# An attention layer's Z projection as seven products, exponentials, last gate group and row factors moved, on one Trainium2 core

## What is computed

```python
h = rms_norm(x, g_mix)
(qa, ka, va, za, beta_in, a_in, qd, kd, vd, gate_a, gate_b) = split(h @ w_in)
qa, ka, va = silu(causal_depthwise_conv([qa, ka, va], conv_w))        # then l2-normalised q, k
oa = rms_norm(gated_delta_rule(qa, ka, va, beta, g), g_delta_out) * silu(za)
qd, kd = rms_norm(qd, q_norm), rms_norm(kd, k_norm)
od = rms_norm(diff_attention(qd, kd, vd, lam, rel_bias), g_subln) * (1 - lam_init)
mix = sigmoid(gate_a + b_gate[0]) * oa + sigmoid(gate_b + b_gate[1]) * od
x = x + mix @ w_o
x = x + moe_ffn(rms_norm(x, g_ffn), w_router, ..., w_up, w_down, ...)  # top 4 of 32, clamped SwiGLU
```

## Time and profile before

| | |
|---|---|
| median of three runs | 1276.15 us |
| profiled execution | 1277.58 us |
| its span (first to last instruction) | 1275.9 us |
| TensorE, matmuls | 1220.6 us, 96% of the span |
| VectorE | 391.1 us, 31% |
| ScalarE | 308.3 us, 24% |
| GpSimd | 43.3 us, 3% |
| moved by DMA | 465.59 MB, 365 GB/s over the span |
| chain that ended last | TensorE 65%, DMA 19%, VectorE 5%, ScalarE 3% |

### The profile page before, as it was taken

One profiled execution on the slowest core, in us unless ns is written; L12 is line 12 of the kernel. 1 busy time (PEld: TensorE's weight loads), 2 busy tenths in 40 slices (PEclk: granted clock), 3 DMA queues, 4 the chain that ended last, 5 costly groups with the idle time before them and its releaser, 6 DMA issues.

```text
span 1275.9 us, 14962 instructions
## 1 busy us (share of the span) xinstructions
PE 1220.6 (96%) x5558; PEld 535.2 (42%) x5558; DVE 391.1 (31%) x1041; ACT 308.3 (24%) x644; POOL 43.3 (3%) x100
## 2 busy tenths in 40 slices
PE   9999999999999999999999999999999999999997
PEld 7777456644443333333333333333333333333332
DVE  5776647479341221111221111221111112211111
ACT  3332222464222121121121112121121211111121
POOL 4401000000000000000000000000000000000000
PEclk9999999999999999999999999999999999999999
DMA  7644974698969999999999999999999999999997
GB/s 257 185 156 131 226 234 150 156 299 303 380 257 423 426 429 428 429 428 428 428 429 427 429 429 429 428 428 427 429 429 428 428 427 429 428 429 428 429 426 303
DMA packets 67582, 465.59 MB, mean 365 GB/s; under 512 B 11016, under 2 KB 14216, under 8 KB 42848
## 3 DMA queue, kind: packets, MB, share of 16 engines
q1 hardware_dynamic: 61768, 452.68, 86.1%
q0 software_dynamic: 5344, 11.95, 4.9%
q10 hardware_dynamic: 440, 0.58, 0.1%
HBM read 462.84 MB, written 1.97 MB: 364 GB/s over the span
## 4 chain that ended last, share of the span: by engine, by line
PE 65%; DMA 19%; DVE 5%; ACT 3%; issue 2%; SPq 1%; DVEq 0%; ACTq 0%
PE pb L2037 20%; DMA space<-in_w_up_dram 19%; PE pb L2084 14%; PE pb L1747 6%; PE pb L1978 4%; PE pb L1698 4%; PE pb L1678 3%; PE pb L1965 3%; PE pb L1892 2%; PE pb L1653 2%; PE pb L1972 1%; PE pb L1997 1%; DVE buf_a L1592 1%; DVE buf_a L1589 1%; DVE buf_a L1586 1%
## 5 line engine op out<-in xcount | busy, mean ns | idle before, releaser
L2037 PE MATMUL pb<-space,buf_a 128*64 128x512 f32 x2048 | 460.4, 595 | 16.1 <-DMA space<-in_w_up_dram 16.1
L2037 PEld LDWEIGHTS pb<-space,buf_a 128*64 128x64 f32 x2048 | 146.1, 137 | 285.3 <-issue 257.2
L1586 DVE TENSOR_SCALAR buf_a<-pb 128x256 f32<-128x256 f32 x64 | 26.9, 421 | 687.2 <-PE pb L2037 687.2
L2084 PE MATMUL pb<-space 128*64 128x512 f32 x1024 | 227.1, 595 | 7.3 <-ACT space L1114 7.3
L2084 PEld LDWEIGHTS pb<-space 128*64 128x64 f32 x1024 | 70.7, 137 | 140.9 <-issue 125.3
L1090 ACT ACT_TABLE_LOAD x32 | 41.1, 1283 | 222.4 <-PE pb L1965 222.4
L1678 PE MATMUL pb<-space 128*128 128x256 f32 x384 | 88.6, 384 | 1.0 <-ACT space L924 0.6
L1107 ACT ACTIVATE buf_a<-buf_a 128x256 f32<-128x256 f32 x64 | 26.7, 417 | 217.3 <-DVE buf_a L1586 217.3
L1678 PEld LDWEIGHTS pb<-space 128*128 128x128 f32 x384 | 71.3, 190 | 13.2 <-issue 2.4
L1116 ACT COPY space<-pb 128x512 f32<-128x512 f32 x32 | 18.7, 585 | 209.9 <-PE pb L2084 209.9
L1978 PE MATMUL pb<-space 64*128 64x512 f32 x264 | 65.6, 615 | 0.8 <-ACT space L1116 0.8
(11 more groups left out here) (322 smaller groups left out, 949.7 us busy)
## 6 DMA issues: line engine op xcount, KB each, us to landing
space<-in_w_up_dram SPq DMA_DIRECT2D x127, 2048.0 KB, 24.9
space<-in_w_down_dram SPq DMA_DIRECT2D x61, 2048.0 KB, 23.3
space<-in_w_in_dram SPq DMA_DIRECT2D x25, 1024.0 KB, 7.3
space<-in_w_in_dram SPq DMA_DIRECT2D x7, 2048.0 KB, 11.1
space<-in_w_in_dram POOLq DMA_DIRECT2D x8, 1024.0 KB, 10.7
space<-in_w_o_dram SPq DMA_DIRECT2D x4, 1024.0 KB, 5.2
space<-in_w_down_dram SPq DMA_DIRECT2D x4, 1024.0 KB, 29.2
xt<-in_x_dram SPq DMA_DIRECT2D x4, 512.0 KB, 8.9
```

The source lines that it names most:

```text
L1586: v.tensor_scalar(glu[:, cols], pairs[:, :, 0], LIMIT, None, ALU.min).then_inc(s_glu, 1)
L2037: ins = mm(up_out(hf, n_), xg[:, c, :], up_columns(line, hf, n_), start=False, stop=(c == KC - 1), skip_group_check=True)
L2084: ins = mm(pb[64 * hf:64 * hf + 64, 2, :], actT[:, c // 4 * 2 + c % 2, hf_in, :], slot(m)[:, at_:at_ + 512], start=(c == 0), stop=(c == KC ...
```

## The change

- Z joins `SEVEN`. Its products go in the order P5 P1 P3 P6 P2 P7 P4, in banks 0 and 1. ScalarE takes the products P5, P3, P1 and P7 out of PSUM, times 0.25, into `gz`, VectorE adds or subtracts the others (`results_step`, L1266 to L1279), ScalarE takes the tanh of each output and VectorE forms the product. Its weights are loaded as those of the other groups, with one first sum, one third sum and two growing sums. The list of products is one shorter (43 in place of 44), Z at index 22, GA at 29, GB at 36.
- `PLACES`, `BANKS` and `W_O_PLACES` have new entries; GA and GB use banks 0 to 3 in another order, and the quarters of `w_o` lie in other halves of slots 8 and 9. SP's order of loads follows. Slot 9 is freed with slot 8, at the fourth product of the output projection.
- Every item of the delta rule stands one index later, and so do attention's items and `odn`.
- The exponentials are an item of their own, `ex`, one index behind the scores and, on ScalarE, behind the copy of the turned weights of the head before.
- `odn`: ScalarE multiplies each block and head with its rows' factor (twelve and four operations, L1010), then VectorE multiplies with the gain, one operation a row block (L1454).
- GB goes in the order P5 P1 P2 P6 P3 P7 P4, with outputs ready in the order of `LAST_OUTS` (2, 1, 0, 3), so both of b = 0 first; the mixed rows' second half of b = 0 is turned ahead of P4 and the first half behind it.
- SP waits for GB's P7 before it loads `xt`.

```diff
 UNITS = ("P5", "P1", "P7", "P6", "P3", "P2", "P4")
+Z_UNITS = ("P5", "P1", "P3", "P6", "P2", "P7", "P4")
+LAST_UNITS = ("P5", "P1", "P2", "P6", "P3", "P7", "P4")
 HALVES = tuple((b, n, hf) for n in range(2) for b in range(NB) for hf in range(2))
-SEVEN = (KD, VD, GA, GB)
-SEQ = [(g, name) for g in range(6) for name in (UNITS if g in SEVEN else HALVES)]
+SEVEN = (KD, VD, Z, GA, GB)
+SEQ = [(g, name) for g in range(6) for name in {QD: HALVES, Z: Z_UNITS, GB: LAST_UNITS}.get(g, UNITS)]
...
 BANKS = {KD: {"P5": 0, "P3": 0, "P1": 7, "P6": 7, "P7": 6, "P4": 6, "P2": 1},
          VD: {"P5": 0, "P3": 0, "P1": 1, "P6": 1, "P7": 6, "P4": 6, "P2": 7},
-         GA: {"P5": 0, "P3": 0, "P1": 2, "P6": 2, "P7": 3, "P4": 3, "P2": 1},
-         GB: {"P5": 0, "P3": 0, "P1": 1, "P6": 1, "P7": 3, "P4": 3, "P2": 2}}
+         Z: {"P5": 0, "P3": 0, "P2": 0, "P4": 0, "P1": 1, "P6": 1, "P7": 1},
+         GA: {"P5": 2, "P3": 2, "P1": 3, "P6": 3, "P7": 1, "P4": 1, "P2": 0},
+         GB: {"P5": 2, "P3": 2, "P1": 0, "P6": 0, "P7": 1, "P4": 3, "P2": 3}}
...
 PLACES = {KD: {"T": (6, 0), "T3": (6, 1), "B11": (8, 0), "B22": (8, 1), "B21": (9, 0)},
           VD: {"T": (9, 1), "T3": (6, 1), "B11": (8, 0), "B22": (8, 1), "B21": (9, 0)},
-          Z: {(0, 0): (6, 0), (1, 0): (8, 0), (0, 1): (6, 1), (1, 1): (8, 1)},
-          GA: {"T": (9, 0), "T3": (6, 0), "B11": (9, 1), "B22": (8, 0), "B21": (8, 1)},
-          GB: {"T": (6, 1), "T3": (6, 0), "B11": (9, 1), "B22": (8, 0), "B21": (8, 1)}}
-W_O_PLACES = {(0, 0): (9, 0), (0, 1): (9, 1), (1, 0): (8, 0), (1, 1): (8, 1)}
+          Z: {"T": (6, 0), "T3": (6, 1), "B11": (8, 0), "B22": (8, 1), "B21": (9, 0)},
+          GA: {"T": (9, 1), "T3": (6, 1), "B11": (8, 0), "B22": (8, 1), "B21": (9, 0)},
+          GB: {"T": (6, 0), "T3": (6, 1), "B11": (8, 0), "B22": (8, 1), "B21": (9, 0)}}
+W_O_PLACES = {(0, 0): (9, 1), (0, 1): (8, 0), (1, 0): (9, 0), (1, 1): (8, 1)}
...
+Z_OUTS, LAST_OUTS = (1, 2, 0, 3), (2, 1, 0, 3)
...
-put(12, ("n2", 0))
...
+put(13, ("n2", 0))
...
 for h in range(H):
-    put(19 + 2 * h, ("a1", h))
-    put(21 + 2 * h, ("aw", h))
-    put(22 + 2 * h, ("a2", h))
-    put(23 + 2 * h, ("a3", h))
-put(35, ("odn", 0, 6))
-put(38, ("odn", 6, 8))
+    put(20 + 2 * h, ("a1", h))
+    put(21 + 2 * h, ("ex", h))
+    put(22 + 2 * h, ("aw", h))
+    put(23 + 2 * h, ("a2", h))
+    put(24 + 2 * h, ("a3", h))
+put(36, ("odn", 0, 6))
+put(39, ("odn", 6, 8))
...
-    after[i].sort(key=lambda it: {"aw": 0, "a2": 0, "grow": 1, "a1": 3}.get(it[0], 2))
-put(43, ("mt", 0), ("mt", 1))
+    after[i].sort(key=lambda it: {"aw": 0, "a2": 0, "grow": 1, "a1": 3, "ex": 3}.get(it[0], 2))
+put(41, ("mt", 1))
+put(42, ("mt", 0))
...
-sp.wait_ge(s_wo, {9: 3, 8: 4}[i])
+sp.wait_ge(s_wo, 4)
...
-load_quarter(Z, (0, 0))
+begin_sum(Z)
 after_product(VD, "P1")
-load_quarter(Z, (1, 0))
+load_quarter(Z, "B11")
 after_product(VD, "P7")
-load_quarter(Z, (0, 1))
+begin_third_sum(Z)
 after_product(VD, "P3", 1)
-load_quarter(Z, (1, 1))
+load_quarter(Z, "B22")
 after_product(VD, "P2", 2)
+load_quarter(Z, "B21")
+after_product(VD, "P4")
 begin_sum(GA)
-after_product(VD, "P4")
+after_product(Z, "P1")
 load_quarter(GA, "B11")
-after_product(Z, (1, 0, 1))
+after_product(Z, "P3", 1)
+load_quarter(GA, "B22")
+after_product(Z, "P2", 2)
+load_quarter(GA, "B21")
+after_product(Z, "P7")
 begin_third_sum(GA)
-load_quarter(GA, "B22")
 front_dead(0)
 load(0)
-after_product(Z, (1, 1, 1))
-load_quarter(GA, "B21")
+after_product(Z, "P4")
 begin_sum(GB)
 front_dead(1)
...
+after_product(GB, "P2", 2)
+load_w_o(1, 0)
 after_product(GB, "P3", 1)
-load_w_o(1, 0)
-after_product(GB, "P2", 2)
 load_w_o(1, 1)
 load(4)
+after_product(GB, "P7")
 for b in range(NB):
     sp.dma_start(xt[:, b, :], x[0, b * P:(b + 1) * P, :]).then_inc(s_x[b], 16)
...
+Z_USED = {"P2": (1, 1), "P7": (2, 2), "P4": (0, 3)}
+LAST_USED = {"P2": (2, 1), "P3": (1, 3), "P7": (0, 4), "P4": (3, 5)}
...
+act_e.wait_ge(s_gd, 4 if it[1] == 0 else 6)
+for b in range(NB):
+    for h in range(it[1], it[2]):
+        ins = sc.activation(OD_h[:, b, h], OD_h[:, b, h], ACT.Copy, scale=rsd[:, b, h:h + 1])
+ins.then_inc(s_gd, 1)
...
+if g == Z and (g, name) in taken:
+    act_e.wait_ge(s_pj, done[(g, name)])
+    if name == "P5":
+        act_e.wait_ge(s_red, 2)
+    b, n_ = OUTS[{"P5": 0, "P3": 1, "P1": 2, "P7": 3}[name]]
+    sc.mul(gz[:, b, 512 * n_:512 * n_ + 512], pb[:, BANKS[g][name], :], 0.25).then_inc(s_pjf, 1)
...
-elif it[0] == "a1":
+        use(SEVEN[turn_of(g) - 2], 3, 5)
+    elif name == "P5" and g == GA:
+        use(Z, 3, 4)
+elif it[0] == "ex":
...
+if g == Z:
+    if name == "P6":
+        dve.wait_ge(s_pjf, taken[(g, "P3")])
+        ins = v.scalar_tensor_tensor(out=c12, in0=src, scalar=-0.25, in1=c12, op0=ALU.mult, op1=ALU.add)
+    elif name == "P2":
+        ins = v.scalar_tensor_tensor(out=c11, in0=src, scalar=0.25, in1=c11, op0=ALU.mult, op1=ALU.add)
+    elif name == "P7":
+        dve.wait_ge(s_pjf, taken[(g, "P7")])
+        ins = v.tensor_tensor(c22, c22, c21, ALU.subtract)
+    else:
+        dve.wait_ge(s_cf, results(g, 3))
+        ins = v.scalar_tensor_tensor(out=c21, in0=src, scalar=0.25, in1=c21, op0=ALU.mult, op1=ALU.add)
+    ins.then_inc(s_cf, 1)
+elif g == GB:
+    if name == "P2":
+        dve.wait_ge(s_pjf, taken[(g, "P1")])
+        ins = v.tensor_tensor(c11, src, c11, ALU.add)
+    elif name == "P6":
+        dve.wait_ge(s_gm, 8)
+        v.tensor_tensor(c12, gate_bias(g, 1), src, ALU.subtract)
+        v.tensor_tensor(c22, c22, src, ALU.subtract)
+        ins = v.tensor_tensor(c21, gate_bias(g, 3), src, ALU.add)
+    elif name == "P3":
+        dve.wait_ge(s_cf, results(g, 2))
+        ins = v.tensor_tensor(c12, src, c12, ALU.add)
+    elif name == "P7":
+        v.tensor_tensor(c21, c21, src, ALU.add)
+        ins = v.tensor_tensor(c22, c22, src, ALU.subtract)
+    else:
+        dve.wait_ge(s_cf, results(g, 4))
+        ins = v.tensor_tensor(c21, src, c21, ALU.add)
+    ins.then_inc(s_cf, 1)
...
+dve.sem_inc(s_gd, 1)
 if lo == 0:
     dve.wait_ge(s_bup, 1)
+dve.wait_ge(s_gd, 5 if lo == 0 else 7)
 for b in range(NB):
-    for h in range(lo, hi):
-        ins = v.scalar_tensor_tensor(out=OD_h[:, b, h], in0=OD_h[:, b, h], scalar=rsd[:, b, h:h + 1], in1=gsubr, op0=ALU.mult, op1=ALU.mult)
+    ins = v.tensor_tensor(OD_h[:, b, lo:hi], OD_h[:, b, lo:hi], gsubr[:, None, :].to_broadcast([P, hi - lo, P]), ALU.mult)
...
+elif g == GA and name in ("P5", "P1"):
+    gate_product(Z, 0 if name == "P5" else 3)
...
-pe.wait_ge(s_mix, OUTS.index((b, n_)) + 1)
+pe.wait_ge(s_mix, LAST_OUTS.index(OUTS.index((b, n_))) + 1)
 if b:
-    pe.wait_ge(s_mixT, n_ + 1)
+    pe.wait_ge(s_mixT, 2 - n_)
```

145 lines of the change are left out of this document (71 added, 74 removed).

## The result

The changed kernel takes 1288.83 us (median of 1288.83, 1289.65 and 1287.65), 1.0091 times the kernel before, 95% interval 1.0075 to 1.0108: slower by 12.7 us by the medians, 11.6 by the ratio. Forecast was 1275.1, no change that can be told, in a range to 1279.5.

A forecast was written before the change was run, and what follows sets the result against it. It took the start of the continuous weight stream, set by the output projection and VectorE's line ahead, as the bound. Projection -3.3 to -1.6 us and slot 9 +1.4 gave a middle of -1.1: 1275.1 us, range 1268.5 to 1279.5.

The forecast's parts named there:

- The last group's order: GB's end: only b = 0's two quarters needed, mixed quarter to projection 5.1 to 6.8 us against 9.2, -4.1 to -2.4.
- The first hole and the keys' factors: TensorE at 163 and behind L1371: 2.53 us hole, 1.7 of clock and 1.4 wait go, 5.6 us in all.
- The wait at VD's P7: TensorE at about 184 waits about 1.4 us for VD's third sum; Z's sixth product still begins 6.3 us earlier.
- The wait at GA's P7: GA's third sum, loaded only after Z's P7, lands near 268.6 after 13.6 us; TensorE waits 3.2 us.
- VectorE's line: VectorE's work from Z's last product to the first mixed quarter: five terms give +0.8 us, ready at 323.0 instead of 322.2.
- holes of over 8 us in VectorE: Sign between 255 and 320: such holes would show the forecast wrong, with the kernel faster.
- The 326.5 to 328.5 among the signs: Expected start of the output projection in the profile after the change; it was 329.8 before.
- Slot 9: Output projection: slots 8 and 9 both wait for the fourth product, so the weight stream stands later, cost 1.4 us.
- The exponentials: Attention: three TensorE waits for the weights' copy, 5.0 us, vanish; nothing further credited, since VectorE is the next thing late.
- The slow one: Rival: ScalarE's pass ahead of the last group becomes the bound, at head 7's a3 and P6; 1278.9 us, chance 0.22.
- The fast one: Rival: GA's third sum takes 8.6 us, no wait, VectorE catches up; 1267 to 1273 us, chance 0.38.
- That nothing reaches the stream: Rival: slabs behind slots 8 and 9 catch up whatever the projection gains; 1276 us, chance 0.1 of the forecast's 0.40.

The follow-up runs named there:

- e6: Changed kernel with the first quarter of VD's third sum issued right behind the inverse's block transfers and Z's first quarter held until VD's P1: ratio 1.0045.
- e2: Changed kernel with GA's and GB's third sums swapped with their B11 quarters in the ring, so loaded earlier: ratio 1.0029 to the kernel before.
- e9: Changed kernel with its last group in the old order of the kernel before, banks, loads, results and turns with it: ratio 1.0080.
- e8: Kernel before with only the exponentials moved one product later, behind ScalarE's copy of the previous head's turned weights: ratio 0.9949.
- e13: e11 with the row factors of heads 0 to 5 one index later, behind VectorE's taking of GB's P1: ratio 0.9946.
- e3: Changed kernel with the attention rows' factors back on VectorE as in the kernel before: ratio 1.0066.
- e12: e11 with the attention rows' factors on ScalarE as the change has them: ratio 1.0013 to the kernel before.
- e14: Changed kernel with the row factors of heads 0 to 5, still on ScalarE, one index later, behind the taking of GB's P1: ratio 1.0065.
- e11: Changed kernel with four edits together, those of e2, e3, e6 and e9: ratio 0.9980, median 1274.5 us.
- e15: Kernel before with the exponentials moved, all steps one product later and VD's third sum first behind the blocks' transfers: ratio 0.9934.
- e1: Changed kernel with the load for VD's third sum moved ahead of the wait for the inverse's diagonal blocks: ratio 1.0129.

## Why the prediction was wrong

The forecast was -1.1 us. The step that failed is what TensorE loses to late third sums: 1.4 and 3.2 us of waits were forecast, with no lower clock in the sum; measured were 3.94 and 5.34, and 2.9 and 1.6 more for the lower clock behind them. With it failed the path. I held that VectorE's work in line decides; in the changed kernel the late sums did, and VectorE had 16.8 us of holes from 255 to 320. The last group's order, counted as a gain of 2.4 to 4.1 us, brought none that shows. By the forecast's own steps:

- **The first hole and the keys' factors.** Right. No hole at 163, the step at about half of its 3.42 us, no wait of 1.4 us. But TensorE stood 1.1 us later at 151.99 than before at the same place, in a stretch that the change doesn't touch; it lies in how that run went.
- **The wait at VD's P7.** Failed in size: 1.4 us forecast, 3.94 measured, and 2.9 more since the product took 6.45 us instead of 3.60 (the timeline's length for a product). I took the middle of 8.6 and 13.6 for the landing, 11.1, from two other transfers; it was 13.0. The same transfer in the kernel before, the one at 174.17, took 12.2 us there, which would have made the wait 2.5:

```profile
space<-in_w_in_dram POOLq DMA_DIRECT2D x1, 1024.0 KB, 12.2
```

  The sum was also issued 1.7 us later than in that row, and TensorE came 1.1 later. I charged no clock for a wait, though the earlier trace rows show a lower one behind the hole at 163. So the landing was 3.6 us late and the clock took 2.9: Z's sixth product began at 251.91 instead of 245.8, and the lead of 6.3 us was all but gone. e6 gives 5.9 us back.
- **The wait at GA's P7.** Right in mechanism, short in size: 3.2 forecast, 5.34 and 1.6 of clock measured. Load and TensorE were both late by the 6.2 us of the step above, which leaves the wait as it is; the transfer took 15.6 us instead of 13.6, and that is the difference. Z's P7 to GA's P7 was 16.1 us for TensorE, as forecast. e2 gives it back. By the Trainium skill, SBUF — State Buffer, "SBUF: two separate sides", POOL could not have written this transfer's descriptors while VectorE ran an operation like L1514 in its two-port mode. The rows leave little room for that: the line is busy 1.09 us inside the 15.6 us and not at all inside the 13.0 us at VD, which was slow as well.
- **VectorE's line.** By GA's P7 the lateness was 9.9 us (281.9 against 272.0). From there my terms came near: the factors on ScalarE +3.3 (7.16 against 4.82 us for six heads, 3.60 against 2.62 for two) where I had +3.1; the stand for P6 4.4 where I had 2.3. The first mixed quarter came at 334.8, not 323.0: 9.9 and 2.1, less 0.2 elsewhere. The sign "VectorE busy over 66 of the 75 us from 254" measured 53.9, and the other, that holes of over 8 us in VectorE mean a faster kernel, pointed the wrong way: it had twice that and the kernel was slower.
- **The last group's order.** From the first mixed quarter to the projection 7.7 us, not 5.1 to 6.8: the turn at the lower clock 1.1, P4 4.5, and a wait of 1.6 for ScalarE's copy of the second turn, which stood behind the tanh of P4's result. That order between the two was not seen. Against the 9.2 us of the kernel before this is still 1.5 less in the traces; the runs of e9 show no gain. The 326.5 to 328.5 among the signs is not what the forecast's terms give: 323.0 and 5.1 to 6.8 are 328.1 to 329.8, since 1.6 of the gain was clock and not start.
- **Slot 9.** Cost at most 0.9 us, not 1.4 (381.5 less 380 is 1.5 by the forecast's own terms): by the rule above, kernels with the old place lie at 944.1 to 944.4 and those with the new one at 944.4 to 945.0.
- **The exponentials.** The step "I credit nothing for them" failed the other way: e8 shows 6.5 us. VectorE was not the next thing late in the kernel before; in e13, with Z's sums on it, it is.
- **The rivals.** The slow one (ScalarE's pass, chance 0.22) was named for the right place, and e3 and e12 put 3 to 5 us on it, but it is only a part of the loss. It had the lower clock at P6 and P4, and the text names it as an "or" at GA's P7; at VD's P7 nothing has it. The fast one (0.38) needed GA's sum in 8.6 us, and it took 15.6. That nothing reaches the stream is refuted by the rule above: a later projection is paid in full.

**The account.** For the profiled pair the miss adds up: 11.8 us at the first mixed quarter (6.2 from VD's sum, 3.7 from GA's, 2.1 from the stand for P6, less 0.2), 1.7 from there to the projection against the middle of the forecast, less 1.2 at slot 9, make 12.3, from -1.1 to +11.2.

The runs price the parts alone: VD's late sum 5.9 us, GA's 7.9, the row factors 3.2 to 4.2, their place ahead of the taken P1 3.3 (e14), the last group's order 1.4, each uncertain by 2 to 3. They overlap: the four edits of e11 gave 18.4 us alone and 14.2 together. With e13's move on top it is 18.5, from 11.6 above the kernel before to 6.9 below it, which is about what the exponentials alone give there (6.5). So undoing these five gives back the loss and what hid the exponentials' gain, and neither the earlier steps nor the product saved in Z (3.45 us) shows in the time: e13, with it, is no faster than e15, without it, though the two differ in more than that. No run has Z's seven products alone in the kernel before, so their own price is open.

## What to carry to other kernels

When an engine is made to reach a point earlier, look for the next transfer that it needs there and ask whether that was issued earlier too. Here TensorE was to gain 5.6 us and lost 6.8 at a transfer whose issue had not moved; take its length from its own row, not from others of its kind. Charge a wait on TensorE with the clock behind it as well (up to 2.9 us here). Test a bundled change part by part: one of its parts was worth -6.5 us, another cost 3 to 5, and two late transfers cost more than both.

## What the runs showed of the hardware

- An adding transfer of 1 MB from POOL's queue took 8.3 to 9.3 us where the DMA engines moved 142 to 248 GB/s over its stretch and 12.2 to 15.6 where they moved 238 to 326, with SP's quarters or slabs beside it. That is an observation over ten transfers in the changed kernel and eight in the one before, and one pair (e1). The two ranges of rates meet, so the rate alone does not tell how long it takes. VectorE's work does not tell it either: a transfer of 8.6 us at 125.44 in the kernel before had VectorE busy for 7.9 of them, the one of 12.2 us at 174.17 for 4.2.
- The clock did not always fall behind a hole, nor by its length. After 3.94 and 5.34 us in the changed kernel and 7.22 in e1 the next eight or sixteen matmuls took 2.9, 1.6 and 1.8 us longer (against 3.60 and 1.95); after 3.63 in e2 and 5.72 in e6 1.8 and 2.4; after 2.53 us in the kernel before 1.5, but after 2.27 us in e8 the same step ran at 2.02 us, next to its usual 1.95:

```profile
165.46 2.02 PE L1654 MATMUL pb<-space 128*128 128x128 f32 x16 [2.27 <-issue]
```

- What makes that difference is open.
